# One of four blocks of a 31-tap convolution, moved from VectorE to products with diagonal matrices on TensorE

## The reference, cut to what matters

```python
ga, gg = jnp.split(glu, 2, axis=-1)
u = ga * jax.nn.sigmoid(gg)
u = causal_dwconv(u, conv_b_w, conv_b_b)      # width 31, one filter for each channel
b_out = jax.nn.silu(layernorm(u, ln_b_g, ln_b_b))
x = x + jnp.concatenate([a_out, b_out], axis=-1) @ w_out
```

## Time and profile before

| | |
|---|---|
| median of three runs | 1432.0 us |
| profiled execution | 1433.88 us, of it the span from first to last instruction 1432.1 us |
| TensorE matmuls busy | 1378.1 us (96%) |
| VectorE busy | 787.3 us (55%) |
| ScalarE busy | 539.4 us (38%) |
| GpSimd busy | 606.6 us (42%) |
| the attention's steps 0 to 25 | about 129 to 219 us of the span |

### The profile page before, as it was taken

The page is one execution under the profiler, slowest core; times in us unless marked ns, Lnnn a source line. Parts: engine busy times, 40 slices in busy tenths (PEclk is TensorE's granted clock), DMA queues, the critical chain, the costliest instruction groups (busy, mean ns, idle before and its releaser), DMA issues.

```text
span 1432.1 us, 18114 instructions
## 1 busy us (share of the span) xinstructions
PE 1378.1 (96%) x6240; PEld 1097.8 (77%) x6240; DVE 787.3 (55%) x1077; ACT 539.4 (38%) x843; POOL 606.6 (42%) x295
## 2 busy tenths in 40 slices
PE   7999999999999999999999999999999999999997
PEld 5687766877678888888888777677778888888885
DVE  6698984262366777777633588655463333333232
ACT  4445666343343232332323254434343233233221
POOL 3587971242134444444444443111234444444341
PEclk8999988899999999999999999999999999999999
DMA  6122320122122222222222222111122323233321
GB/s 218 50 91 81 106 72 30 55 85 67 44 74 88 89 101 96 95 103 99 101 101 95 88 74 75 44 45 45 45 76 101 100 90 103 89 107 101 102 87 73
DMA packets 31874, 121.18 MB, mean 85 GB/s; under 512 B 3536, under 2 KB 3664, under 8 KB 31568
## 3 DMA queue, kind: packets, MB, share of 16 engines
q1 hardware_dynamic: 31392, 119.55, 24.7%
q10 hardware_dynamic: 432, 0.96, 0.3%
HBM read 118.40 MB, written 2.10 MB: 84 GB/s over the span
## 4 chain that ended last, share of the span: by engine, by line
PE 75%; issue 13%; POOL 5%; DVE 2%; ACT 2%; DMA 1%; POOLq 0%; SPq 0%; DVEq 0%; ACTq 0%
PE acc L1613 60%; POOL weights_low L588 3%; PE acc L1761 3%; POOL conv L637 2%; PE aux L1983 2%; PE acc L1733 1%; PE aux L1847 1%; PE aux L2003 1%; PE aux L1828 1%; PE aux L1985 1%; PE aux L1836 1%; DMA weights_raw<-w 1%; PE aux L1993 1%; PE aux L1667 0%; PE aux L2019 0%
## 5 line engine op out<-in xcount | busy, mean ns | idle before, releaser
L588 POOL TENSOR_TENSOR weights_low<-weights_raw,weights_high 128x1024 fp32r<-128x1024 f32 (+1 forms) x204 | 525.0, 2574 | 795.9 <-ACT weights_high L665 792.8
L665 ACT CAST weights_high<-weights_raw 128x1024 fp32r<-128x1024 f32 (+1 forms) x202 | 222.1, 1099 | 519.4 <-PE acc L1613 498.2
L1613 PE MATMUL acc<-a_high,weights_high 128*128 128x512 f32 x976 | 389.5, 399 | 5.6 <-POOL weights_low L588 3.0
L1613 PE MATMUL acc<-a_high,weights_low 128*128 128x512 f32 x976 | 381.8, 391 | 0.0
L1613 PE MATMUL acc<-a_low,weights_high 128*128 128x512 f32 x976 | 381.6, 391 | 0.0
L1613 PEld LDWEIGHTS acc<-a_high,weights_high 128*128 128x128 f32 x976 | 184.2, 189 | 49.5 <-issue 7.6
L1613 PEld LDWEIGHTS acc<-a_low,weights_high 128*128 128x128 f32 x976 | 184.2, 189 | 38.9 <-issue 2.1
L1613 PEld LDWEIGHTS acc<-a_high,weights_low 128*128 128x128 f32 x976 | 184.1, 189 | 38.7
L1119 DVE TENSOR_TENSOR residual<-acc,residual 128x512 f32<-128x512 f32 (+1 forms) x56 | 38.5, 688 | 183.2 <-PE acc L1613 145.0
L1613 PE MATMUL acc<-h_high,weights_high 128*128 128x512 f32 x352 | 137.8, 391 | 0.0
L1613 PE MATMUL acc<-h_high,weights_low 128*128 128x512 f32 x352 | 137.2, 390 | 0.0
(11 more groups left out here) (339 smaller groups left out, 1894.0 us busy)
## 6 DMA issues: line engine op xcount, KB each, us to landing
weights_raw<-w SPq DMA_DIRECT2D x172, 512.0 KB, 3.2
weights_raw<-w SPq DMA_DIRECT2D x32, 704.0 KB, 4.0
residual<-xT SPq DMA_DIRECT2D x8, 256.0 KB, 7.2
out<-y_tok SPq DMA_DIRECT2D x4, 512.0 KB, 3.7
mem_raw<-memT SPq DMA_DIRECT2D x1, 1024.0 KB, 5.4
mem_tok<-mem SPq DMA_DIRECT2D x1, 1024.0 KB, 7.5
lru_weights<-blockdiag ACTq DMA_DIRECT2D x1, 512.0 KB, 3.3
sine<-positions ACTq DMA_DIRECT2D x1, 256.0 KB, 6.9
```

What stands on the lines that cost most here:

```text
L588: g.tensor_tensor(weights_low[:, s, 0:cols], weights_raw[:, s, 0:cols], weights_high[:, s, 0:cols].bitcast(F32), ALU.subtract).then_inc(we ...
L665: a.copy(weights_high[:, s, 0:cols], weights_raw[:, s, 0:cols]).then_inc(weight_high, 1)
L1613: last = t_.matmul(acc[:, bank, 0:cols], w[:, s, wide], x_[:, k0 + k, 0:cols], start=start and k == opens and n == 0, stop=stop and k == c ...
```

## The change

Block 3 leaves VectorE. `CONV` keeps 53 taps (block 2, and the 22 of block 1) in steps 0 to 15. In steps 16 to 25 TensorE makes block 3 as 31 products accumulated in `aux[5]`: for tap `k`, ScalarE writes a 128 x 128 matrix with the tap's weights on its diagonal into one of four buffers (the identity times a column of weights), and TensorE multiplies it with `glu[:, 3, k:k+T]`, in fp32. There are three products a step, four in step 25. When they are done, ScalarE copies `aux[5]` with the bias to `conv[:, 3]`, and "mean" waits for that copy also.

```diff
+        diagonal = sb("diagonal", [P, 4, P], where=s1b)
...
-        CONV = [(n, k) for n in (2, 3) for k in range(TAPS)] + [(1, k) for k in range(SHARED_TAPS, TAPS)]
+        CONV = [(2, k) for k in range(TAPS)] + [(1, k) for k in range(SHARED_TAPS, TAPS)]
...
-        CONV_STEPS, PRODUCT_STEPS = 25, 24
+        CONV_STEPS, PRODUCT_STEPS, FIRST_DIAGONAL, LAST_DIAGONAL = 16, 24, 16, 25
...
+            if FIRST_DIAGONAL <= step <= LAST_DIAGONAL:
+                steps = LAST_DIAGONAL + 1 - FIRST_DIAGONAL
+                FIRST_PLAN += [("diagonal", k) for k in range((step - FIRST_DIAGONAL) * TAPS // steps,
+                                                              (step + 1 - FIRST_DIAGONAL) * TAPS // steps)]
...
-            if step == 25:
-                FIRST_PLAN.append(("mean",))
+            if step == LAST_DIAGONAL:
+                FIRST_PLAN += [("diagonal_out",), ("mean",)]
...
# ScalarE
+                elif what == "diagonal":
+                    act.wait_ge(params_in, 16)
+                    if j >= 4:
+                        act.wait_ge(diagonal_used, j - 3)
+                    a.activation(diagonal[:, j % 4], ident[:], ACT.Copy, scale=col("conv_w", 3 * TAPS + j)
+                                 ).then_inc(diagonal_ready, 1)
+                elif what == "diagonal_out":
+                    act.wait_ge(diagonal_used, TAPS)
+                    a.activation(conv[:, 3], aux[5][:], ACT.Identity, bias=col("conv_b", 3)
+                                 ).then_inc(diagonal_out, 1)
...
# TensorE
+                elif what == "diagonal":
+                    pe.wait_ge(diagonal_ready, j + 1)
+                    if j == 0:
+                        pe.wait_ge(conv_steps, len(CONV))
+                        pe.wait_ge(glu_ready, 4)
+                    t_.matmul(aux[5][:], diagonal[:, j % 4], glu[:, 3, j:j + T], start=j == 0,
+                              stop=j == TAPS - 1).then_inc(diagonal_used, 1)
                 elif what == "mean":
                     pe.wait_ge(conv_steps, len(CONV))
+                    pe.wait_ge(diagonal_out, 1)
```

More of the change, by code:

```diff
@@ L261, in build @@
         glu_clear = sem("glu_clear")
+        diagonal_ready = sem("diagonal_ready")
+        diagonal_used = sem("diagonal_used")
+        diagonal_out = sem("diagonal_out")
         angle_ready = sem("angle_ready")
```

## The result

The changed kernel takes 1468.5 us (four runs, 1465.9 to 1471.5) against 1432.1 (four runs too); the ratio is 1.0256, 95% interval 1.0236 to 1.0276. It is 36.4 us slower.

What follows compares the result with a forecast made beforehand. TensorE was taken to bound steps 16 to 25: 29.1 own work + 27.3 products + 10.3 waits = 66.7 us against 36.0, 30.7 more. That gave 1464.6 us profiled, 1462 us median; range 1451 to 1470.

Steps and rivals of the forecast that it cites:

- The bound: Steps 16 to 25: TensorE sets the pace; VectorE is full but not late, so removing its taps gains nothing itself.
- The rival in which VectorE was the pace: Steps 16 to 24 give back VectorE's 24.2 us; with one-pass products 15.4 us less, 1417 us; chance 0.03.
- no change: Steps 16 to 25: products at 0.73 us, or one-pass products without VectorE gain, 1434 us; chance 0.03.
- The products: Steps 16 to 25: 31 fp32 products on TensorE at 0.88 us each add 27.3 us.
- the price by passes, 28.5 us: Alternative count for the 31 products: four passes through the array, 0.92 us each, 1.2 more than the term used.
- The waits: Steps 16 to 25: TensorE waits for ScalarE's diagonals, and for the copy before "mean"; 10.3 us, bounds 1.7 and 13.6.
- the rival that I had given 0.22: New clock fall, as behind step 17's 2.3 us wait: 10 us low, 5 us lost, 1467 us; chance 0.22.
- The range: Whole kernel: 1451 to 1470 us, the main case with the nearer parts of the next two.
- my main case: Whole kernel: no new clock fall, waits as summed, 1462 us, within 1455 to 1466; chance 0.57.
- the sum of 1464.6: Forecast for the profiled execution: 1433.9 us plus 30.7 us more in steps 16 to 25.
- The 6.9 us taken as gone: Steps 16 to 25: idle time and half clock near step 18 vanish, 36.0 us becoming 29.1 before additions.
- a sign of being wrong: Steps 0 to 15 or the stretch behind "mean" taking a different time, or products following at clearly under 0.8 us.

Runs made afterwards that it cites:

- experiment 2: Changed kernel with only the product of tap 0 left, in step 25, and the other 30 taps of block 3 left out: 1437.8 us, ratio 1.0041.
- experiment 3: Changed kernel with 31 VectorE instructions added in steps 16 to 25, one beside each product, written to an unread tile: 1469.1 us, ratio 1.0264.
- experiment 1: Changed kernel with ScalarE making the diagonals one step earlier, in eight buffers instead of four, products in place: 1455.5 us, ratio 1.0168.
- experiment 6: Changed kernel with diagonals made one step earlier, fp32, only taps 0 to 15 of block 3, other 15 left out: 1443.9 us, ratio 1.0083.
- experiment 5: Changed kernel with diagonals made one step earlier and products in fp32r, low parts of both operands left out: 1437.3 us, ratio 1.0034.
- experiment 7: Kernel before, all 84 taps on VectorE, with the 30 shared ScalarE and GpSimd products moved in the plan: 1431.1 us, ratio 0.9993.
- experiment 8: Changed kernel with fp32 products moved to steps 1 to 10, diagonals a step ahead, VectorE's 53 taps in steps 11 to 24: 1458.5 us, ratio 1.0174.
- experiment 9: Changed kernel with fp32r products in steps 1 to 10, diagonals a step ahead, VectorE's 53 taps in steps 11 to 24: 1440.6 us, ratio 1.0053.
- experiment 4: Changed kernel with products in fp32r from a rounded copy of block 3, diagonals made where the changed kernel makes them: 1457.1 us, ratio 1.0175.

## Why the prediction was right, and where it was off

*The bound.* That TensorE, not VectorE, sets the pace of steps 16 to 25 is shown by experiments 2 and 3: 31 taps less changed 33.91 us by nothing, 31 instructions more changed 70.4 us by nothing. The rival in which VectorE was the pace, and "no change", are gone with them.

*The products.* Forecast 27.3 us at 0.88; experiment 1 has 0.88 a product net, and from one product to the next it is 0.86 (experiment 6). In the changed kernel itself three products take 2.77 us, 0.92 each, because the first comes out of a wait, but four take 0.86 more than three (records of 3.70 and 2.84), so the pace is the same. That 0.92 is also the price by passes, 28.5 us, is chance; experiment 5 bears out that passes make nearly all of the price, at 0.20 and not 0.23 us each.

*The waits.* Forecast against measured, steps 16 to 25: 0.7 and 0.79, 2.3 and 2.31, 0.35 and 0.47, 1.2 and 0.97, 0.85 and 0.93, 0.25 and 0.25, 0.85 and 0.92, 1.2 and 0.97, 0.25 and 0.25, 1.4 and 1.21; before "mean" 0.95 and 0.82. Sum 10.3 and 9.9. Adding up the queue ahead of the diagonal, operation by operation, was enough.

*What was mis-sized.* The stage came to 70.4 us, not 66.7. Of the missing 3.7, 1.7 are the rival that I had given 0.22: the clock did fall behind the wait in step 17, for 3.4 us and not 10, so that it cost a third of the price I had set. Another 2.1 are what the ten waits cost beyond their records, 0.2 each (experiment 1); my sum took a wait to end where the product starts. Against these stand 0.4 of waits that I had too long, and 0.3 are left that I can't place.

*Where it was luck.* The range held, but not my main case: the median of 1468.5 lies outside the 1455 to 1466 of the forecast and in the band of the rival, 1466 to 1472, and it did not get there as the rival says, since the fall cost 1.7 us and not 5. That it happened in step 17 was itself open: experiment 3 has the same wait without it, and one fall of the same length elsewhere. The profiled execution, 1465.9 us, lies only 1.3 above the sum of 1464.6, but because 3.7 us too little in the stage met 2.4 us that went away outside it. The rest of the distance to the median is the run that was taken as the base: I had taken off 1.9 us, as the profiled execution before was slower than the median, while the changed kernel's is 2.6 us quicker than its own; 0.7 is rounding. A part of the 2.6 can be the fall of the clock at 28 us, which the trace before has and this one has not (1.7 us); the other three runs left no trace, so that is not shown.

*The 6.9 us taken as gone.* Gone they were, and for the reason given: with longer steps the fill of step 18 found its `vc` copies done, and its logits begin at full clock at 198.25. But experiment 7 shows that this sum was not as safe as I took it: 5 of the 6.9 us were a fall of the clock, and when the load shifts a shorter one and new waits come at other places.

*Outside the stage.* I had called it a sign of being wrong if steps 0 to 15 or the stretch behind "mean" took another time. Steps 0 to 15 took 0.4 us longer (54.4 in experiments 1 and 2 too), where I had counted nothing; the stretch behind "mean" took 1.2 less, and where that comes from I did not find.

## What to carry to other kernels

Before work is moved to a second engine, look whether the first one is waited for: an engine busy 97% of a window was worth nothing here, since the engine beside it followed start on start. Count for the receiving engine not only the instruction, but the place of its operand in the producer's queue: a third of the loss went when the matrices were made one step earlier. A stall costs more than its record shows, 0.2 us each here. It can also be paid in clock, but which stall pays could not be told from its length, and a fall avoided at one place may come at another.

## What the runs showed of the hardware

The run-to-run spread goes with the clock: over four runs of the changed kernel the span rises from 1464.1 to 1469.7 us while the mean granted clock falls from 0.985 to 0.981. That is 12 us more at half clock, 6 us lost, against 5.6 measured. Thirteen runs of the kernel before, beside experiments 8 and 9, go from 1427.9 us at 0.986 to 1438.1 at 0.977.

The length of a gap did not decide whether TensorE's clock fell. The wait of 2.31 us in step 17 was followed by 0.50 in the changed kernel and by 1.00 in experiment 3, where the fall came behind one of 0.97. The gap of 2.81 to 2.85 us that ends at about 28.5 us is in all eleven traces; at or behind it the clock fell in eight and stayed at 1.00 in three (the changed kernel, experiments 6 and 9). Gaps of 2.09 us (experiment 8, at 135.17) and 2.64 us (experiment 9, at 134.25) left it at 1.00; 1.33 us (experiment 4, at 187.84), 1.21 us (experiment 2) and the 1.92 us of the kernel before were followed by a fall. The low stretches lasted from 3.4 us (1.7 us lost) over 10 us to 13.6 us (experiment 9).

An fp32 product of 128 x 128 with 512 columns costs 0.86 us from one to the next in a dense stream (experiment 6), one in fp32r 0.27 us or less (experiment 5). Three fp32 products take 0.2 us more, beyond the recorded wait, where the first comes out of one (experiment 1). ScalarE makes a 128 x 128 diagonal in 0.39 us, and one every 0.3 us when they stand in a row.
